# A two-layer hybrid block: first loads, first products, the HGRN ladder and a few fills in another order

## The reference

```
mod = silu(c) @ w_mod[l] + b_mod[l]            # 6 rows of 1024, and the same from c_ctx
h = rms_norm(x, norm1_g[l]) * (1 + sc1) + sh1
p = split_cols(h @ w_in[l])                    # columns of the four branches and of the gates
o = sum_n sigmoid(gate_n) * (branch_n @ w_branch[n])
x = x + g1 * (o @ w_out[l])
x = x + g2 * (square(relu(modulate(x) @ w_ff1)) @ w_ff2)
```

## Time and profile before

| what | value |
|---|---|
| three timed runs | 1590.11, 1590.38, 1596.29 us |
| median | 1590.38 us |
| the profiled execution, its own time | 1596.18 us |
| its span, first to last instruction | 1594.4 us |
| mean granted TensorE clock | 0.989 of full speed |

### The profile page before, as it was taken

How to read it: one execution, slowest core, us unless ns; L and a number is a source line. 1 busy time by engine, 2 the same in 40 slices (tenths; PEclk the granted TensorE clock), 3 DMA queues, 4 the chain that set the end, 5 groups by cost and what they waited for, 6 DMA issues and landing times.

```text
span 1594.4 us, 23959 instructions
## 1 busy us (share of the span) xinstructions
PE 1544.5 (97%) x9994; PEld 1273.0 (80%) x9994; DVE 918.4 (58%) x1448; ACT 640.9 (40%) x957; POOL 207.5 (13%) x174
## 2 busy tenths in 40 slices
PE   5999999999999999999999999999999899999999
PEld 3788777776557768888888888888888668999999
DVE  4787457635543225588655554686276574575553
ACT  6622343243443224453124322543255554464452
POOL 0100002223001110031002200000014301122130
PEclk9999999899999999999999999999999999999999
DMA  9421232022121142346555565131332323455553
GB/s 386 193 79 58 87 146 109 27 88 67 66 86 67 60 172 106 133 172 224 194 202 185 185 211 179 59 109 54 114 124 97 114 93 133 166 187 184 185 186 106
DMA packets 36763, 214.86 MB, mean 135 GB/s; under 512 B 3952, under 2 KB 7408, under 8 KB 12720
## 3 DMA queue, kind: packets, MB, share of 16 engines
q1 hardware_dynamic: 36656, 213.34, 37.9%
HBM read 211.23 MB, written 2.10 MB: 134 GB/s over the span
## 4 chain that ended last, share of the span: by engine, by line
PE 89%; DVE 5%; DMA 2%; ACT 2%; issue 1%; POOL 0%; SPq 0%; DVEq 0%; ACTq 0%
PE ps L1111 10%; PE ps L1109 10%; PE ps L1110 10%; PE ps L555 10%; PE ps L557 10%; PE ps L556 10%; PE ps L533 6%; PE ps L745 2%; PE ps L939 2%; PE ps L566 2%; PE ps L567 1%; PE ps L568 1%; DMA arena<-in_w_mod 1%; PE ps L1054 1%; PE ps L674 1%
## 5 line engine op out<-in xcount | busy, mean ns | idle before, releaser
L557 PE MATMUL ps<-parts 128*128 128x512 f32 (+1 forms) x960 | 332.0, 346 | 0.0
L1111 PE MATMUL ps<-parts 128*128 128x512 f32 (+1 forms) x960 | 322.6, 336 | 0.0
L1109 PE MATMUL ps<-parts 128*128 128x512 f32 (+1 forms) x928 | 311.8, 336 | 0.0
L1110 PE MATMUL ps<-parts 128*128 128x512 f32 (+1 forms) x928 | 311.8, 336 | 0.0
L1878 DVE TENSOR_TENSOR parts<-ring,parts 128x1024 fp32r<-128x1024 f32 x124 | 150.1, 1252 | 138.7 <-ACT parts L1433 138.7
L1433 ACT ACTIVATE parts<-ring 128x1024 fp32r<-128x1024 f32 x124 | 124.4, 1051 | 242.8 <-PE ps L1111 236.9
L557 PEld LDWEIGHTS ps<-parts 128*128 128x128 f32 x960 | 183.2, 191 | 23.3
L555 PE MATMUL ps<-parts 128*128 128x512 f32 (+1 forms) x544 | 195.5, 359 | 3.8 <-issue 1.7
L1111 PEld LDWEIGHTS ps<-parts 128*128 128x128 f32 x960 | 182.2, 190 | 18.6
L1110 PEld LDWEIGHTS ps<-parts 128*128 128x128 f32 x928 | 176.2, 190 | 18.2
L1109 PEld LDWEIGHTS ps<-parts 128*128 128x128 f32 x928 | 176.2, 190 | 18.0
(11 more groups left out here) (294 smaller groups left out, 2463.4 us busy)
## 6 DMA issues: line engine op xcount, KB each, us to landing
ring<-in_w_ff SPq DMA_DIRECT2D x64, 1024.0 KB, 4.8
ring<-in_w_in SPq DMA_DIRECT2D x60, 1024.0 KB, 4.9
ring<-in_w_mod_rows SPq DMA_DIRECT2D x31, 1024.0 KB, 4.8
arena<-in_w_mod SPq DMA_DIRECT2D x8, 1024.0 KB, 21.0
ring<-in_w_branch SPq DMA_DIRECT2D x32, 256.0 KB, 5.2
ring<-in_w_out SPq DMA_DIRECT2D x8, 1024.0 KB, 5.0
arena<-in_w_mod_rows SPq DMA_DIRECT2D x5, 1024.0 KB, 9.9
ring<-in_w_mod SPq DMA_DIRECT2D x4, 1024.0 KB, 4.9
```

Of the source, the lines that this page charges most:

```text
L557: last = pe.matmul(ps[0:m, 0:n], w_lo[:, k, c], x_hi[:, k, 0:n], start=False, stop=(k == KD - 1))
L1109: pe.matmul(ps[:, 0:nt], w_hi[:, k, c], x_hi[:, k, 0:nt], start=(k == 0), stop=False)
L1110: pe.matmul(ps[:, 0:nt], w_hi[:, k, c], x_lo[:, k, 0:nt], start=False, stop=False)
L1111: last = pe.matmul(ps[:, 0:nt], w_lo[:, k, c], x_hi[:, k, 0:nt], start=False, stop=(k == kt - 1))
```

## The change

It joins several edits.

- **Loads.** The condition row is loaded on one partition (8 KB), then X, then tables and parameters, then the first halves of `hff` and `hfb`, then three pairs of `w_mod`, then the second halves, then the rest. Each has a semaphore of its own.
- **Condition row.** ScalarE makes SiLU of 1x2048; TensorE spreads it over the partitions with a row of ones (four products of 512 columns), VectorE copies it out of PSUM. The load of 1024 KB, the two sigmoids and the GpSimd work are gone.
- **Squares.** VectorE adds squares in four pairs, TensorE sums the four pairs in four matmuls instead of one.
- **First products.** `first_rows` of a pair moves behind the first eight matmuls of its step, `first_columns` behind the whole step; four warm-up products stand ahead of the first step. Weights are split by halves.
- **Small ones.** The retention decays (four table loads on ScalarE) move from the start to behind `mlstm_gates`; the lower bounds behind the first norm. VectorE takes the low part of `hv` before dots 9 to 11 (and, in the second layer, before the gates). ScalarE copies `hv` out of PSUM instead of VectorE.
- **Ladder.** Levels 1 and 2 are woven: each product writes its columns where they belong, both directions in one bank in two turns with a wait between them; VectorE places whole rows of 128x512. `busy` is gone between levels 128 and 256, and the projection of FILL[128] takes its place (`hgrn_far`).
- **Fills.** `mlstm_rows` moves ahead of `branch_features(HG)` and has tiles of its own; a Tanh of `merge` goes ahead of a weight split; MLA queries go ahead of keys; `mla_turn` goes between retention's scores and values.

```diff
+            def condition_rows():
+
+                for q in range(4):
+                    ps = bank(("crow", q), fixed=q - ROTATING)
+                    pe.wait_ge(*s_sil.at("row"))
+                    pe.matmul(ps[:, :], ones_row, crow_row[:, q * T:(q + 1) * T], start=True, stop=True)\
+                        .then_inc(*product.up(("crow", q)))
...
+            def warm(n):
+
+                for i in range(n):
+                    pe.matmul(PS[ROTATING - 1][:, 0:256], tab("ident"), tf[:, 0:256], start=True, stop=True)
...
+                    warm(4)
                 for k in range(KD):
                     pair = k // 2 + 1 if l == 0 and k % 2 == 0 and k // 2 + 1 < FIRST else None
-                    if pair:
-                        first_rows(pair)
                     pe.wait_ge(*s_h.at(("h", l, 0, k)))
                     for ps, name, j in tiles:
                         w_hi, w_lo = [w[:, k, j * P:(j + 1) * P] for w in split(l, ("in", name))]
@@ -674,7 +689,7 @@
                         pe.matmul(ps[:, :], w_hi, M_HI[:, k, :], start=(k == 0), stop=False)
                         pe.matmul(ps[:, :], w_lo, M_HI[:, k, :], start=False, stop=False)
                     if pair:
-                        first_columns(pair)
+                        first_rows(pair)
...
-                    pe.wait_ge(*s_sum.at(("sum", l, w, KD - 1)))
-                    pe.matmul(ps[:, 0:n], tab("ones"), ACC[:, 0, 0:n], start=True, stop=True)\
-                        .then_inc(*product.up(("ss", l, w, 0)))
+                    for k in range(1, KD, 2):
+                        pe.wait_ge(*s_sum.at(("sum", l, w, k)))
+                        last = pe.matmul(ps[:, 0:n], tab("ones"), ACC[:, k - 1, 0:n], start=(k == 1), stop=(k == KD - 1))
+                    last.then_inc(*product.up(("ss", l, w, 0)))
...
+            def hgrn_woven(l, L):
+
+                nch = 4 if l == 0 else 2
+                group = 8 // nch
+                pe.wait_ge(*s_hd.at(("late", l, L)))
+                pe.wait_ge(*s_hd.at(("early", l, L)))
+                for j in range(HEADS // group):
+                    pair = [bank(("hl", l, L, half, j)) for half in range(2)]
+                    for turn_over in range(2):
+                        for i in range(4):
+                            for x in range(2):
+                                for d in range(2):
+                                    half = d ^ turn_over
+                                    if turn_over and i + x == 0:
+                                        pe.wait_ge(*product.at(("woven", l, L, j, 1 - d)))
+                                    h, c = divmod(group * nch * j + 4 * half + i, nch)
+                                    y = 64 * (x ^ d)
+                                    a = c * P + y
+                                    q = query(d, h, a, 64).rearrange("p (b two t) -> p b two t", two=2, t=L)[:, :, 1 - d, :]
+                                    o = pair[half][y:y + 64, P * i + y:P * i + y + 64]
+                                    o = o.rearrange("p (b two t) -> p b two t", two=2, t=L)[:, :, 1 - d, :]
+                                    if L == 1:
+                                        q, o = q[:, :, 0], o[:, :, 0]
+                                    last = scores(o, d, h, a, 64, q)
+                                    if i == 3 and x:
+                                        last.then_inc(*product.up(("hl", l, L, half, j) if turn_over else ("woven", l, L, j, d)))
+
             def hgrn_level(l, L):
+                if L < 4:
+                    hgrn_woven(l, L)
+                    return
...
-                busy(("cross", l), 6)
+
+            def hgrn_far(l):
...
@@ -983,9 +1032,9 @@
                 pe.wait_ge(*s_rv.at(("rot", l, 1)))
                 retention_scores(l, 0)
                 merge(l, ML, [6])
+                for j in range(2):
+                    mla_turn(l, 1, j)
                 retention_values(l, 0)
-                for j in range(2):
-                    mla_turn(l, 1, j)
                 retention_scores(l, 1)
                 merge(l, ML, [7])
                 retention_values(l, 1)
...
+                spread(("qlb", l), aroot[:, 4:8], nq)
                 spread(("kvb", l), aroot[:, 0:4], 4)
-                spread(("qlb", l), aroot[:, 4:8], nq)
...
                 fill(FILL[128])
+                hgrn_far(l)
...
-            sp.dma_start(csv, io["c"]).then_inc(s_const.sem, 16)
-            sp.dma_start(par[:, :], io["params"]).then_inc(s_const.sem, 16)
-            sp.dma_start(tf[:, :], io["tables"]).then_inc(s_const.sem, 16)
+            sp.dma_start(csv, io["c"]).then_inc(s_cond.sem, 16)
+            sp.dma_start(crow_row, io["c_rows"][0:1]).then_inc(s_crow_mixer.sem, 16)
...
+            sp.dma_start(tf[:, :], io["tables"]).then_inc(s_tab.sem, 16)
+            sp.dma_start(par[:, :], io["params"]).then_inc(s_par.sem, 16)
+            for i in range(2):
+                _, _, src = sources(plan[i])[0]
+                sp.dma_start(ring[:, i * SLOT:i * SLOT + 1024], src[:, 0:1024]).then_inc(s_half[i].sem, 16)
             load_first(0)
-            load(0)
-            load(1)
             load_first(1)
             load_first(2)
+            for i in range(2):
+                _, _, src = sources(plan[i])[0]
+                sp.dma_start(ring[:, i * SLOT + 1024:i * SLOT + 2048], src[:, 1024:2048]).then_inc(loaded[i].sem, 16)
             load_first(3)
...
-            sp.dma_start(unit(38, 4), io["c_rows"]).then_inc(s_crow_mixer.sem, 16)
...
+            def first_high(x):
+
+                for i, name in enumerate(("hff", "hfb")):
+                    sem = (loaded if x else s_half)[i]
+                    act.wait_ge(sem.sem, 16)
+                    c = slice(1024 * x, 1024 * (x + 1))
+                    act.activation(high_of(("in", name))[:, c], ring[:, i * SLOT:i * SLOT + 2048][:, c], ACT.Copy)\
+                        .then_inc(*s_mh.up(("w", 0, ("in", name), x)))
...
-            def condition_row_gates():
-
-                act.wait_ge(s_crow_mixer.sem, 16)
-                for s in range(2):
-                    act.activation(crow_gate[s], crow_mixer[:, s, :], ACT.Sigmoid).then_inc(*s_row_gate.up(s))
...
+                    gate_first = n == ML and m == 0
...
+                    if gate_first:
+                        part_high(l, next_part(("gate", n, m // 2)))
...
                 gate_rows(l)
                 mlstm_gates(l)
+                if l == 0:
+                    retention_decays()
                 part_high(l, ("in", "rv"))
...
-                    for k in range(1, KD):
-                        sum_square(l, w, k)
+                    for k in range(1, KD, 2):
+                        dve.wait_ge(*s_sq.at(("sq", l, w, k)))
+                        dve.tensor_tensor(ACC[:, k - 1, :], ACC[:, k - 1, :], ACC[:, k, :], ALU.add)\
+                            .then_inc(*s_sum.up(("sum", l, w, k)))
...
+                    for q in range(4):
+                        ps = read(dve, ("crow", q))
+                        freed(("crow", q), "mixer_condition_rows", q)
+                        dve.tensor_copy(unit(38 + q), ps[:, :]).then_inc(*s_row_mixer.up(q))
+                    part_low(l, ("in", "hff"), [0])
+                    part_low(l, ("in", "hfb"), [0])
+                    dve.wait_ge(s_par.sem, 16)
                     first_modulation(0)
...
+                        if L < 4:
+                            natural = PT[l].rearrange("p h c t -> p (h c) t")[:, 8 * j + 4 * d:8 * j + 4 * d + 4]
+                            dve.copy_predicated(natural, pair_mask[:, i * P:(i + 1) * P].unsqueeze(1).broadcast_to([P, 4, P]),
+                                                ps[:, :].rearrange("p (x t) -> p x t", x=4)).then_inc(*s_hp.up(("pt", l, L, d, j)))
+                            continue
...
-                dve.wait_ge(*s_ov.at(("on", HG, l, 1)))
                 ps = read(dve, ("lT", l, 0))
                 freed(("lT", l, 0), "mlstm_vector", ("grow", l))
-                dve.tensor_copy(SQ[rows, 0, :], ps[rows, :]).then_inc(*s_lv.up(("grow", l)))
+                dve.tensor_copy(LROWS, ps[rows, :]).then_inc(*s_lv.up(("grow", l)))
...
+                    lower_bounds()
                 part_low(l, ("in", "hq"))
+                if l == 0:
+                    mixer_dot(8)
+                part_low(l, ("in", "hv"))
+                if l == 0:
+                    dve.wait_ge(*s_sil.at("lb"))
...
+                mlstm_rows(l)
+                branch_features(HG, l)
                 if l == 0:
+                    retention_decays()
...
-                branch_features(HG, l)
-                mlstm_rows(l)
...
-                pool.wait_ge(*s_row_gate.at(s))
-                pool.tensor_tensor(crow_mixer[:, s, :], crow_mixer[:, s, :], crow_gate[s], ALU.mult)\
-                    .then_inc(*s_row_mixer.up(s))
```

141 lines of the change are left out of this document (74 added, 67 removed).

## The result

| | before | after |
|---|---|---|
| timed runs on the first chip, us | 1589.88 to 1596.29 (5) | 1561.26 to 1567.65 (5) |
| median, us | 1590.38 | 1562.05 |
| span of the profiled execution | 1594.4 | 1560.0 |
| its mean granted clock | 0.989 | 0.999 |

The changed kernel takes 0.9822 of the time, 95% interval 0.9802 to 0.9843. On a second chip, where it ran six more times beside experiments, it took 0.9857 (0.9830 to 0.9883).

What follows compares the result with a forecast made beforehand. TensorE was taken as the bound: its own work, 50 us of waits and losses at the lower clock. Terms summed to -25.9: 1570.3 from the profiled 1596.2, 1564.5 from the median 1590.4; forecast 1565, range 1556 to 1580.

Steps and rivals of the forecast that it cites:

- start, by the end of the first products: Kernel start: first product at 25.5 instead of 28.5, pair 1's rows now inside, warm-up saving 1.3; net -2.5 us.
- `hq`, `hv` and the clock at 72: First layer: the 1.9 us wait for `hv`'s low part and the 1.6 of half-rate clock behind it go; -3.5.
- retention decays at `rv`: ScalarE's decays, moved ahead of `rv`'s high part, make TensorE wait there; +1.0 us, up to +2.8.
- `mlstm_rows`, both layers, and the clock at 1164: Waits for the copy L2202 behind `branch_features` go in both layers, with 1.7 of clock in the second; -4.9 us.
- Tanh, queries and the clock at 1240: The Tanh's 1.9 us wait and 1.7 of clock go, queries save 0.8; -4.4.
- turn in retention: `mla_turn` between retention's scores and values covers the 1.3 us wait at L975; -1.3.
- The ladder: Weaving levels 1 and 2 shortens VectorE's placing: -1.4 us first layer, -4.55 second with clock; six turns cost +1.3.
- `busy`, both layers: Unread products between ladder levels 128 and 256 go, a projection tile covering VectorE's decays instead; -5.6 us.
- The clock rival: Half-rate stretches behind removed long waits stay, as the clock may follow how densely TensorE works; 1575 us, chance 0.25.
- Waits only move: Whole kernel: TensorE reaches later points earlier and waits there, so only `busy` is gained; 1585 us, chance 0.06.
- The rival with 0.07, the stretch at 304 goes too: The 6.8 us half-rate loss at 304, with no long wait ahead, also vanishes because everything shifts; 1558 us, chance 0.07.
- the slower rival: Woven ladder products run alone, not side by side in the array's quarters; 75 us more, 1640 us, chance 0.05.

Runs made afterwards that it cites:

- e5: The changed kernel run again with no change, as the measure for the runs beside it: median 1567.1 us (six runs, 1561.7 to 1574.7).
- e6: The changed kernel without the four warm-up products ahead of the first step: 1565.3 us.
- e2: The changed kernel with ladder levels 1 and 2 made and placed as before, not woven, in both layers: 1570.2 us.
- e8: The changed kernel with the first turns of both pairs of banks ahead of the second turns in woven levels: 1565.0 us.
- e1: The changed kernel with the six unread `busy` products back between ladder levels 128 and 256 in both layers: 1571.5 us.
- e3: The changed kernel with `mlstm_rows` behind `branch_features` again, and block 14's dots ahead of both in the first layer: 1568.7 us.
- e7: The changed kernel with ScalarE's retention decays behind the high part of `rv` instead of ahead of it: 1564.2 us.
- e4: The kernel before the change with four unread products ahead of each of four long TensorE waits: 1586.9 us against 1588.1, ratio 0.9989.
- e10: The changed kernel with each row of narrow mLSTM value products cut in halves, the next head's scores between them: 1584.6 us.
- e9: The changed kernel with the first half of pair 1's modulation rows in place of the four warm-up products: 1565.8 us.

## Why the prediction was right, point by point

1565 was forecast, with 1556 to 1580 around it; 1562.1 was measured, and 1565.0 over all executions. Each term against the same work in the two profiles (us; negative is earlier):

| term | predicted | measured |
|---|---|---|
| start, by the end of the first products | -2.5 | -2.6 |
| `hq`, `hv` and the clock at 72 | -3.5 | -5.2 |
| ladder, first layer, with turns | -0.5 | -0.5 |
| `busy`, both layers | -5.6 | -5.6 |
| retention decays at `rv` | +1.0 | +1.0 |
| `mlstm_rows`, both layers, and the clock at 1164 | -4.9 | -5.0 |
| Tanh, queries and the clock at 1240 | -4.4 | -3.9 |
| turn in retention | -1.3 | -1.9 |
| ladder, second layer, with turns and the clock at 1068 | -4.1 | -3.8 |
| no term: stretch at 304 | 0 | -5.5 |
| no term: stretch at 364 | 0 | -1.6 |
| sum of the span | -25.9 | -34.4 |

(The measured rows add up to 34.6; small steps the other way are not listed. Without the two stretches that had no term, 27.3 are left of the 34.4.)

- *The start* had the right size by other steps, so its agreement is partly luck. The first product came at 24.1, not 25.5 (25.4 in e5). I had the load of pair 0 on the path, done at 21.0; but both halves of it had landed by 17.2, and TensorE's own work stood ahead of its rows. Spreading the condition row (L641, 7.16) and the four sums (L710, 5.32) did not fall in a time of waiting: TensorE is busy with them without a gap from 4.89 to 17.2, mostly at the low clock, and the rows follow at once. Then L673 waited 1.9 for the copy L1425, where I had 0.4: ScalarE's list has the first weights' high parts (`first_high`) ahead of it, and I had read past them. The warm-up, 1.3 in the sum, is worth 0.4 to 1.4 (e6). In e5 the gain of the start was 2.1.
- *`hq` and `hv`* were mis-sized by 1.7. The short waits for `hq` (0.71 and 0.28), which I left out, went with the rest of VectorE's lateness.
- *The ladder.* e2: weaving gives 0.5 in the first layer and 2.4 in the second. A turn took 0.31, not 0.22, +0.5 us over six. The 0.22 of the earlier trace rows is idle time of the weight loads, which that view counts with the line; in it the turns of the changed kernel are 0.22 each too, but a level gets longer by 0.31 for each. My estimate of 0.13 by the Trainium skill ("TensorE: Matmul & The Clock Gate", "The cost: per-tile semaphore tail") was further off. e8 shows that the cost can be covered.
- *`busy`, rows, decays*: e1 gave 5.6, e3 5.0 with the clock, e7 0.9, each within 0.1 of its term. Cover and late neighbours were read rightly.
- *Tanh and queries* met their number by errors that cancel. The Tanh gave 2.0 and the clock behind it 1.3; the queries gave 2.0 over both layers, not 0.8; and a new wait of 1.37 for VectorE (L2242, at 1213) took 1.3 back. No experiment separates these; they are read from the two profiles.
- *The turn in retention* did not cover the wait that I named. L975's wait of 1.31 stood in the second layer; 1.5 went there, but 1.09 of wait came back at the next such product, so 0.4 was left. The other 1.5 came in the first layer, for which I had no term. The number was luck.
- *The clock rival* is the one that the runs decide most clearly, for the four places behind long waits. e4 removes four stretches by filling waits alone; e2 and e3 bring two of them back with the waits. My support for it, the stretch at 304, was evidence about something else.
- *Waits only move* was wrong for most of the change (e1 and e3: nothing came back) and partly true for e4, which leaves VectorE's list as it is: 3.0 of the 6.9 us came back as waits. In the change itself it happened twice, with the new wait at 1213 and in retention.
- *The rival with 0.07, the stretch at 304 goes too*, is what the profiled execution shows. It need not be an effect of the change: such stretches stand in five later profiles of kernels derived from the changed one, and e4, derived from the kernel before, has none there. This is why the profiled spans differ by 34.4 and the medians by 28.3, and why going by the median was the better choice. "One more half-rate stretch like that at 304" as the 5.8 between profile and median is consistent with e5's runs, not shown.

The woven products paired as hoped; the slower rival needed 84 ns for each and had 16 (e8).

## What to carry to other kernels

A wait of TensorE can have two prices: its length and, for most of those of 1.9 us and more here, the half-rate stretch behind it; the second is saved already when the wait is only shortened (0.78 in place of 2.21 was worth 3.0 us in e2). Before filling such a wait with products that nobody reads, ask which engine was late: unless its list is shortened too, it may be just as late at the next meeting, as at three of e4's four places. Before calling a wait the cause of a slow stretch, look which of the two began first (e10). Where the clock differs between executions of one kernel, compare the start times of the same work, not two medians.

## What the runs showed of the hardware

- Over 14 profiles, behind the first products, TensorE had ten waits of 1.90 to 2.70 us. With six of them (four before, one each in e2 and e3) the clock fell to its lower level for some 3 us or more, beginning between 0.2 us before the wait's end and 1.4 us behind it. With one (2.00, in e4) it did not. At the other three, in e10, it had fallen before the wait began. Of 45 waits of 1.20 to 1.50 one had a stretch behind it, in e10 at 1190, where other kernels had one without a wait.
- Half-rate stretches of 3 to 20 us begin without a wait over 1 us ahead, at three places of the program, in some executions and not in others. The runs of e5, one kernel on one chip, lie between 1561.7 us (mean clock 0.999) and 1574.7 (0.990).
- The first rise of the clock comes at 15.3 to 18.1 us in the twelve profiles with the new start (instructions of the sums, L710, start 0.85 us apart before it and 0.43 behind it). The four sums of squares take 5.3 us in the earliest case and 6.6 in the latest, and the first columns start at 21.0 to 22.6, the later the later the rise. In the seven with a rise at 15.3 to 16.6 the clock fell again 1.1 to 1.6 us behind the wait of 1.89 ahead of the columns, though the warm-up (or e9's rows) ran by then; in the four with a rise at 17.3 to 18.1 and a warm-up it did not.
- A product that waits for products issued just ahead of it on TensorE costs 0.31 us; with half a level of other products between them, nothing (e8).
